# A two-model kernel in fp32: the third weight unit of the first mixers is made from x before the norm is known, and the first loads go in pieces

## The reference

```python
h = rms_norm(x, norm_mix[l])     # x * rsqrt(mean(x*x) + eps) * gain, per token
z = h @ w_in[l]                  # q, k, v, f, conv (3), r_q, r_f, r_i, r_g
...
def hgrn2(q, f_logit, i_in, lb): # q = silu(r_q), f_logit = r_f, v = r_i
```

## Time and profile before

| | us |
|---|---|
| median of 3 runs | 2509.11 |
| lowest and highest run | 2505.28 and 2510.32 |
| the profiled execution, its own time | 2507.98 |
| its span, first to last instruction | 2506.2 |
| TensorE busy | 2463.3 (98%) |
| VectorE busy | 1863.2 (74%) |
| ScalarE busy | 1520.1 (61%) |

### The profile page before, as it was taken

One profiled execution on the slowest core, in us unless ns is written; L12 is line 12 of the kernel. 1 busy time (PEld: TensorE's weight loads), 2 busy tenths in 40 slices (PEclk: granted clock), 3 DMA queues, 4 the chain that ended last, 5 costly groups with the idle time before them and its releaser, 6 DMA issues.

```text
span 2506.2 us, 38463 instructions
## 1 busy us (share of the span) xinstructions
PE 2463.3 (98%) x16646; PEld 2220.8 (89%) x16646; DVE 1863.2 (74%) x1635; ACT 1520.1 (61%) x1558; POOL 0.2 (0%) x4
## 2 busy tenths in 40 slices
PE   9999999999999999999999999999999999999998
PEld 8899999887888888888888888998999999899998
DVE  6765557858888889888888888756875565767655
ACT  6563436567777777777777777557653365665433
POOL 0000000000000000000000000000000000000000
PEclk9999999999999999999999999999999999999999
DMA  6335554325999999999999999433444543343552
GB/s 250 135 120 185 184 187 150 135 85 207 369 350 366 357 365 359 363 361 365 353 359 353 368 356 367 168 135 118 152 166 175 198 167 138 118 168 135 186 185 85
DMA packets 83314, 585.25 MB, mean 234 GB/s; under 512 B 9245, under 2 KB 11133, under 8 KB 12613
## 3 DMA queue, kind: packets, MB, share of 16 engines
q1 hardware_dynamic: 83140, 582.73, 62.8%
HBM read 581.64 MB, written 1.05 MB: 232 GB/s over the span
## 4 chain that ended last, share of the span: by engine, by line
PE 85%; DVE 7%; ACT 4%; DMA 2%; issue 1%; DVEq 0%; SPq 0%; ACTq 0%
PE PS L1789 84%; DVE wlo L1058 3%; ACT whi L553 2%; DMA raw<-in_wm 2%; PE PS L2310 1%; PE PS L1993 1%; DVE stat L1190 0%; ACT pb L666 0%; DVE hT L1104 0%; ACT pt L681 0%; DVE lf L1244 0%; DVE pb L1215 0%; DMA xT<-in_xT 0%; DVE xT L1363 0%; DVE yT L1249 0%
## 5 line engine op out<-in xcount | busy, mean ns | idle before, releaser
L1058 DVE TENSOR_TENSOR wlo<-raw,whi 128x2048 fp32r<-128x2048 f32 x550 | 1257.9, 2291 | 376.3 <-ACT whi L553 368.5
L553 ACT ACTIVATE whi<-raw 128x2048 fp32r<-128x2048 f32 x550 | 1051.6, 1913 | 322.0 <-PE PS L1789 289.0
L1789 PE MATMUL PS<-hhi,whi 128*128 128x256 f32 x1984 | 569.7, 287 | 6.3 <-DVE wlo L1058 1.7
L1789 PE MATMUL PS<-hhi,wlo 128*128 128x256 f32 x1984 | 558.2, 281 | 0.0
L1789 PE MATMUL PS<-hlo,whi 128*128 128x256 f32 x1984 | 558.0, 281 | 0.0
L1789 PEld LDWEIGHTS PS<-hhi,whi 128*128 128x128 f32 x1984 | 373.4, 188 | 16.8 <-issue 12.0
L1789 PEld LDWEIGHTS PS<-hlo,whi 128*128 128x128 f32 x1984 | 373.6, 188 | 1.0 <-issue 0.5
L1789 PEld LDWEIGHTS PS<-hhi,wlo 128*128 128x128 f32 x1984 | 373.4, 188 | 0.0
L1789 PE MATMUL PS<-whi,xghi 128*128 128x512 f32 x896 | 358.9, 401 | 2.2 <-DVE wlo L1058 2.0
L1789 PE MATMUL PS<-whi,xglo 128*128 128x512 f32 x896 | 353.8, 395 | 0.0
L1789 PE MATMUL PS<-wlo,xghi 128*128 128x512 f32 x896 | 353.5, 395 | 0.0
(11 more groups left out here) (364 smaller groups left out, 3540.8 us busy)
## 6 DMA issues: line engine op xcount, KB each, us to landing
raw<-in_wm SPq DMA_DIRECT2D x336, 1024.0 KB, 5.6
raw<-in_ws SPq DMA_DIRECT2D x214, 1024.0 KB, 4.8
xT<-in_xT SPq DMA_DIRECT2D x4, 256.0 KB, 7.8
bsum<-in_bsum SPq DMA_DIRECT2D x1, 1024.0 KB
out_T<-hT SPq DMA_DIRECT2D x4, 256.0 KB, 2.5
lmask<-in_lmask SPq DMA_DIRECT2D x1, 512.0 KB
onehot_in<-in_onehot SPq DMA_DIRECT2D x1, 288.0 KB
lbw<-in_lbw SPq DMA_DIRECT2D x1, 256.0 KB
```

Source lines behind the costliest of these rows:

```text
L553: act.activation(whi[s % SPLIT][:], raw[s % RAW][:], ACT.Copy).then_inc(hi_ready, 1)
L1058: dve.tensor_tensor(wlo[s % SPLIT][:], raw[s % RAW][:], whi[s % SPLIT][:].bitcast(F32), ALU.subtract).then_inc(lo_ready, 1)
L1789: return pe.matmul(out, a, b, start=start, stop=stop, skip_group_check=True)
```

## The change

In both first mixers the third unit (r_i) is multiplied with `uhi` and `ulo`, like the first two, into bank 4 instead of bank 6. ScalarE drains it with two activations, one for each 128 tokens, whose scale is the inverse root. The norm sums are issued inside unit two, after its first half, instead of in front of it. The fourth unit is now the one that takes h in pairs as it comes.

In layer 0 unit one is loaded in four pieces of 512 columns, x is issued from ScalarE's queue, units one and two are split in four pieces each with a semaphore per piece, TensorE waits for each piece, ScalarE splits unit two before it makes the squares, the table set of the root is loaded at the start, and `keep_warm` has 22 matmuls.

```diff
--- before.py
+++ after.py
@@ -131,6 +131,8 @@
         v1_loaded, small_loaded, tables_loaded, stored = (
             sem(n) for n in ("v1_loaded", "small_loaded", "tables_loaded", "out_stored"))
         x_loaded = [sem(f"x_loaded{j}") for j in range(DK // 2)]
+        piece_landed = [sem(f"piece_landed{j}") for j in range(DK // 2 - 1)]
+        hi_piece, lo_piece = sem("hi_piece"), sem("lo_piece")
         raw_landed = [sem(f"raw_landed{i}") for i in range(RAW)]
         hi_ready, lo_ready, unit_used = sem("hi_ready"), sem("lo_ready"), sem("unit_used")
         selectors_cast, consts_set, act_chain, dve_chain = sem("selectors_cast"), sem("consts_set"), sem("act_chain"), sem("dve_chain")
@@ -490,6 +492,15 @@
             return out + [Projection(pair(sg, i), func=ACT.Tanh, scale=0.5) for i in range(12)]
 
 
+        def piece(j):
+            return slice(2 * j * UC, (2 * j + 2) * UC)
+
+        def hi_piece_ready(s, j):
+            return (hi_piece, 3 * s + j + 1) if j < DK // 2 - 1 else (hi_ready, s + 1)
+
+        def lo_piece_ready(s, j):
+            return (lo_piece, 3 * s + j + 1) if j < DK // 2 - 1 else (lo_ready, s + 1)
+
         def sync_program(sp):
             def load(s):
                 if s >= RAW:
@@ -500,10 +511,11 @@
                     src = io["ws"][s if s < U_FIRST else s - U_MOE]
                 sp.dma_start(raw[s % RAW][:], src).then_inc(raw_landed[s % RAW], 16)
 
-            load(0)
-            sp.dma_start(v1[:], io["v1"]).then_inc(v1_loaded, 16)
             for j in range(DK // 2):
-                sp.dma_start(xT[:, 2 * j:2 * j + 2, :], io["xT"][:, 2 * j:2 * j + 2, :]).then_inc(x_loaded[j], 16)
+                landed = (piece_landed + raw_landed[:1])[j]
+                sp.dma_start(raw[0][:, piece(j)], io["ws"][0][:, piece(j)]).then_inc(landed, 16)
+                if j == 0:
+                    sp.dma_start(v1[:], io["v1"]).then_inc(v1_loaded, 16)
             load(1)
             load(2)
             load(3)
@@ -552,6 +564,13 @@
                     act.wait_ge(unit_used, s - SPLIT + 1)
                 act.activation(whi[s % SPLIT][:], raw[s % RAW][:], ACT.Copy).then_inc(hi_ready, 1)
 
+            def split_hi_piece(s, j):
+                if s == 0:
+                    act.wait_ge((piece_landed + raw_landed[:1])[j], 16)
+                elif j == 0:
+                    act.wait_ge(raw_landed[s], 16)
+                act.activation(whi[s][:, piece(j)], raw[s][:, piece(j)], ACT.Copy).then_inc(hi_piece_ready(s, j)[0], 1)
+
             def take():
 
                 s = stream.next() - 1
@@ -585,8 +604,9 @@
                     split_x(i, j)
                     square(j)
 
-            def root(bank, columns=False):
-                act.preload_act_table_set("natural_log_exp_and_others")
+            def root(bank, columns=False, loaded=False):
+                if not loaded:
+                    act.preload_act_table_set("natural_log_exp_and_others")
                 after(summed)
                 if columns:
                     step(act.activation(rcol[:, 0:NT], PS[:, bank + 1, 0:NT], ACT.Ln, bias=epsc[:], scale=1.0 / D))
@@ -689,7 +709,7 @@
 
             def first_mixer(l):
                 take()
-                root(0, True)
+                root(0, True, l == 0)
                 after(cols_ready)
                 for t in range(NT):
                     z_t = PS[:, 6, t * UC:(t + 1) * UC]
@@ -706,7 +726,11 @@
                 after(f_clipped)
                 act.activation(lf[:], lf[:], ACT.Ln).then_inc(f_logged, 1)
                 act.activation(lf2[:], lf2[:], ACT.Ln).then_inc(f_logged, 1)
-                out_of(6, flat(ri))
+                act.wait_ge(unit_used, take())
+                for t in range(NT):
+                    ins = act.activation(ri[:, t, :], PS[:, 4, t * UC:(t + 1) * UC], ACT.Copy, scale=rcol[:, t:t + 1])
+                ins.then_inc(drained, 1)
+                C.next(drained)
                 after(rk_turned)
                 act.activation(flat(rk), PS[:, 4, :], ACT.Copy).then_inc(rk_ready, 1)
                 cum_exp()
@@ -1014,14 +1038,19 @@
                         square(j)
                     root(SUMS)
 
+            for j in range(DK // 2):
+                act.dma_start(xT[:, 2 * j:2 * j + 2, :], io["xT"][:, 2 * j:2 * j + 2, :]).then_inc(x_loaded[j], 16)
+            act.preload_act_table_set("natural_log_exp_and_others")
             after(consts_set, 2)
-            split_hi(0)
-            after(v1_loaded, 16)
             for j in range(DK // 2):
+                split_hi_piece(0, j)
+                if j == 0:
+                    after(v1_loaded, 16)
                 split_x(0, j)
             for j in range(DK // 2):
+                split_hi_piece(1, j)
+            for j in range(DK // 2):
                 square(j)
-            split_hi(1)
             first_mixer(0)
             swiglu()
             first_mixer(1)
@@ -1057,6 +1086,11 @@
                 dve.wait_ge(hi_ready, s + 1)
                 dve.tensor_tensor(wlo[s % SPLIT][:], raw[s % RAW][:], whi[s % SPLIT][:].bitcast(F32),
                                   ALU.subtract).then_inc(lo_ready, 1)
+
+            def split_lo_piece(s, j):
+                dve.wait_ge(*hi_piece_ready(s, j))
+                dve.tensor_tensor(wlo[s][:, piece(j)], raw[s][:, piece(j)], whi[s][:, piece(j)].bitcast(F32),
+                                  ALU.subtract).then_inc(lo_piece_ready(s, j)[0], 1)
 
             def take():
 
@@ -1738,13 +1772,14 @@
 
             dve.memset(ones[:], 1.0).then_inc(consts_set, 1)
             dve.memset(epsc[:], EPS).then_inc(consts_set, 1)
-            split_lo(0)
             for j in range(DK // 2):
+                split_lo_piece(0, j)
                 split_x(0, j)
+            for j in range(DK // 2):
+                split_lo_piece(1, j)
             for j in range(1, DK // 2):
                 presum(j)
             presum_out()
-            split_lo(1)
             first_mixer(0)
             swiglu()
             first_mixer(1)
@@ -1800,7 +1835,11 @@
 
             def take():
                 s = stream.next() - 1
-                pe.wait_ge(lo_ready, s + 1)
+                if s < 2:
+                    for j in range(DK // 2):
+                        coming["w", 2 * j] = lo_piece_ready(s, j)
+                else:
+                    pe.wait_ge(lo_ready, s + 1)
                 return whi[s % SPLIT], wlo[s % SPLIT]
 
             def arrive(k):
@@ -1825,6 +1864,7 @@
                 for ks in rounds(first):
                     for f in range(2):
                         for k in ks:
+                            arrive(("w", k))
                             arrive(k)
                             cs = slice(f * P, (f + 1) * P)
                             ins = mm3(PS[:, bank, f * S:(f + 1) * S], wh[:, k, cs], wl[:, k, cs], hi[:, k, :], lo[:, k, :],
@@ -1877,17 +1918,17 @@
                 empty(SUMS, 1, rooted)
                 C.next(h_scaled, 4)
 
-            def first_units(unit1, bank1, freed1, unit2, bank2, freed2, l, columns):
+            def first_units(unit1, bank1, freed1, unit2, bank2, freed2, l, columns, third=None):
 
                 split_in_pairs(u_ready)
                 unit1(bank1, uhi[l], ulo[l], True)
                 empty(bank1, 1, freed1)
-                if columns:
-                    norm_sums(True)
-                    unit2(bank2, uhi[l], ulo[l])
-                else:
-                    unit2(bank2, uhi[l], ulo[l], between=lambda f, k: (f, k) == (0, DK - 1) and norm_sums())
+                unit2(bank2, uhi[l], ulo[l], between=lambda f, k: (f, k) == (0, DK - 1) and norm_sums(columns))
                 empty(bank2, 1, freed2)
+                if third:
+                    unit, bank = third
+                    unit(bank, uhi[l], ulo[l])
+                    empty(bank, 1, drained)
                 C.next(h_scaled, 4)
                 split_in_pairs(h_ready)
 
@@ -2082,9 +2123,8 @@
                 empty(5, 1, hgrn_taken)
 
             def first_mixer(l):
-                first_units(unit_tok, 6, z_sigmoid, unit_T, 7, rows_taken, 0, True)
-                project(unit_tok, 6, True)
-                project(unit_T, 5)
+                first_units(unit_tok, 6, z_sigmoid, unit_T, 7, rows_taken, 0, True, (unit_tok, 4))
+                project(unit_T, 5, True)
                 if l == 0:
                     after(small_loaded, 16 * 11)
                     after(selectors_cast)
@@ -2508,7 +2548,7 @@
                     out_half(4, c, mhi, mlo)
 
             after(consts_set, 2)
-            keep_warm(0, 30)
+            keep_warm(0, 22)
             first_mixer(0)
             swiglu()
             first_mixer(1)
```

## The result

| | before | after |
|---|---|---|
| median, 13 runs each | 2509.61 us | 2517.22 us |
| lowest and highest | 2505.28 to 2511.71 | 2512.85 to 2519.49 |
| ratio, 95% interval | | 1.0029 [1.0021, 1.0038] |
| profiled execution, its own time | 2507.98 | 2518.58 |
| span | 2506.2 | 2516.8 |

The change costs 7.6 us, with an interval of 5.3 to 9.5; forecast were 11 to 12. Start with the page of the profile: the chain's share of PE is higher than in the earlier trace rows, although the kernel is slower, so the page alone does not show the loss.

What follows compares the result with a forecast made beforehand. TensorE bounds the kernel, so what counts is when `keys_turned` starts in each layer. 5.2 (layer 0) + 6.65 (layer 1) = 11.9 on the profiled 2507.98 gives 2520 us (2521 by the median), range 2513.5 to 2523.

Steps and rivals of the forecast that it cites:

- the main case: Late root in both layers, lower TensorE clock behind the gaps: 2520 us, own range 2517.5 to 2522.5, chance 0.48.
- the rival of the fast start: Layer 0: loading in pieces costs the queue nothing, L under 11.2, R 17.9; 2513.6 to 2515.8 us, chance 0.18.
- L: Layer 0: moment unit two's load lands; 13.72 us before, forecast 15.3, between 12.9 and 16.8.
- R: Start of the first activation of `root`: layer 0 19.47 before, forecast 21.95; layer 1 410.76 before, forecast 415.20.
- Layer 1, the root: Layer 1: norm sums behind unit two's wait and half its matmuls make the root start 4.44 us later.
- Layer 1, the bank: Layer 1: transposes of `keys_turned` wait for bank 4 until ScalarE drains `ri`; +5.94 us, +4.2 without this wait.
- Layer 1, the clock: Layer 1: 4.1 us idle before unit four, then clock 0.50 for 5.5 us; unit four takes 8.56, shift +6.65.
- The prediction's remark on the slices of the profile's page: Trace before: the next longest waits, of 1.4 us, left no slice of the page under 9 tenths.
- Layer 0, the start term: Layer 0: root waits for unit two's landing, its split, squares and sums; transposes at 42.98 against 37.75, +5.2 us.
- PE's early start is lost: Layer 0: first pair multiplied from 8.2 instead of 12.10, the lead spent waiting in unit two and before unit four.
- Carried to the end, not absorbed: Both layers' shifts add up to the end; its rival, delay absorbed later by the weight stream: 2508 to 2509, chance 0.07.
- The table load: Layer 0: loading the root's table set at the start is free; up to 3.4 us if data were there sooner.

Runs made afterwards that it cites:

- 3: Kernel after, with the norm sums ahead of unit two again in layer 1: 2510.13 us, ratio 1.0016 to before.
- 5: Kernel after, sums ahead of unit two in layer 1 and `ri` drained before unit five's split in both layers: 2506.43 us, ratio 1.0001 to before.
- 6: Kernel after, with 12 matmuls of ones between units three and four in both layers: 2514.31 us in one run.
- 7: Kernel after, with x issued from SP's queue, each pair behind its piece of unit one: 2514.49 us in one run.
- 9: Kernel before, with `v1` issued behind x: 2506.63 us in one run.
- 2: The new start alone: kernel after, with sums between the units and third unit from h as before: 2508.53 us, ratio 1.0007 to before.
- 10: The new start alone, with squares and their additions ahead of unit two's split: 2506.08 us, ratio 0.9996 to before.
- 1: Kernel before, with only the third unit's part (from x, sums inside unit two, bank 4, scaled drain): 2520.78 us, ratio 1.0053 to before.
- 12: Kernel after, sums ahead in both layers, `ri` drained early, squares first, unit four split right behind the root: 2501.97 us, ratio 0.9983 to before.
- 8: Kernel before, with x issued from ScalarE's queue: 2507.92 us in one run.
- 11: Kernel after, sums ahead of unit two in both layers, `ri` drained before unit five's split, squares first: 2504.06 us, ratio 0.9990 to before.
- 4: Kernel before once more, unchanged, for the spread of its marks: 2507.55 us in one run.

## Why the prediction was right, and what in it was not

The direction and the mechanism held: late sums, a later root, a gap before unit four, the bank held by `ri`. The size did not: the sum was 11.9 and the heads measured 8.1. That the time still fell inside the range is in part luck. 2517.22 lies just under 2517.5, where the main case's own range began, and its +7.6 is of the size that was laid to the rival of the fast start (+5.6 to +7.9). That rival's condition did not come: it needed L under 11.2 and R at 17.9, and they were 12.2 and 19.25. One sign of the main case failed too, the transposes of layer 0 after 41: they came at 39.89. Term by term:

- **Layer 1, the root.** Predicted +4.44, measured +4.50. The sums stand behind unit two's split and half of its matmuls; 3 shows that this place costs 4.28.
- **Layer 1, the bank.** Predicted +5.94 in all, measured +5.98; 3 and 5 show both links.
- **Layer 1, the clock.** Predicted 0.7 on top, measured nothing. The gap of 4.15 did have 0.50 behind it, but for some 3.5 us, not 5.5; unit four was done before `ri`, and 6 has the same 31.76 at the full clock. The step that failed is the length of the low stretch, taken from a single case. In 7 it was 5.3 us behind the same gap, and there the shift was 32.12 - 25.78 = 6.34, near the 6.65: the term is there in some executions and not in others. The prediction's remark on the slices of the profile's page decides nothing for it: the stretch at 0.50 left no slice under 9 tenths either.
- **Layer 0, the start term**, the one mis-sized most: +5.2 predicted, +2.1 measured. L was to be 15.3 and was 12.2, below even my lower bound of 12.9. The upper bound priced 2 KB rows at 181 GB/s; 7 and 9 show that the stretch of the earlier trace rows was slow in part because of `v1`, and that rows of 2 KB alone do not make 181. The lower bound assumed an issue 0.8 sooner and an unchanged time to landing; that time also fell, from 9.9 to 9.1. From L to R I had 6.65 and it was 7.0; from R to unit four 12.47, measured 12.46; unit four at the lower clock 8.56, measured 8.18. So 42.98 - 3.1 + 0.4 - 0.4 = 39.9, as measured.
- **PE's early start is lost**: right. 3.6 us of lead at unit one end as 0.2 at unit four. In 2 what loses it is ScalarE's sitting on unit two, as 10 shows; in the kernel after half of unit two now stands in front of the sums as well.
- **Carried to the end, not absorbed**: right. The ratios of 1, 2, 3 and 10 to 12 follow the shifts of the heads within their intervals or at their edge (+12.3, +1.2, +4.1, -1.8, -0.2 and -4.8, measured +13.3, +1.8, +4.0, -1.0, -2.5 and -4.3 by their ratios). Kernel 5 has +2.0 in its layer 0 and +0.3 measured, inside its interval of 2.3 to either side. The single times of 8 and 9 (+3.1 and +0.6 by the heads, +0.1 and -1.2 measured) can't tell.
- **The table load** was free, as said. What taking it away from the root saves, no run isolates.

**Left open.** What else slows the transfers between 5 and 8 us: the earlier trace rows has 181 GB/s there, 7 and 9 still 242 and 240, and two queues 323 and 346. Also why the lower clock comes behind one idle stretch and not behind a longer one, and why it lasts as long as it does; and where the 2.7 us between the heads of the kernel after come from.

## What to carry to other kernels

Work made independent of a late value gains only if the next thing on the path does not still wait for that value: here unit four's split was queued behind the whole chain of the root, and until it moved (12) freeing unit three only turned work into idle time. Before moving small sums behind a big unit, look at what that unit waits for, and before reusing a buffer earlier, look at where its reader stands in its engine's order. A lead won at the start is kept only if no engine on the path is then made to sit on a later load.

## What the runs showed of the hardware

- The length of an idle stretch does not decide by itself whether TensorE's clock falls. Idle stretches of 2.06 us (11), 3.12 and 3.28 (8 and 2, in the first 20 us) and 3.86 and 4.15 (after) had a granted clock of 0.50 behind them. In the two heads those of 1.87 us (3) and less kept 1.00, but so did 2.35 (9), 2.72 (4) and 2.84 (1), all three ahead of unit one in layer 0. The idle stretch near 1570 us stands in every kernel: with 2.26 us in 10 the clock fell behind it, with 2.25 us in 5 it did not:

```profile
1571.00:1577.00 6.00, 5.86 (x50) 5.86 (x51) 5.02 (x11) 4.76 (x8) 0.00 (x0) 1.00 0.38 109
```

- Once the clock had fallen it stayed at 0.50 for about 3.4 us in some cases (layer 1 of the kernel after and of 1, layer 0 of 7, 8 and 11) and about 6.8 in others (layer 0 of the kernel after and of 1, layer 1 of 7, near 1570 in before), counted from its fall, which can come before the engine restarts. The same gap in the same order had either. The forecast had taken one length for all.
- 104 KB of vectors in short rows, issued ahead of x instead of behind it, delayed the 1 MB behind both by 1.0 to 1.6 us.
- Two executions of the kernel before, 0.03 apart at 1307 us, are 2.8 apart at 1639. The distance from unit one to the transposes in layer 1 repeats to 0.01 in three kernels with the same order there (31.76 in after and 6, 31.75 in 1), and is 32.12 in 7, where the lower clock lasted longer.
